# A two-block transformer layer: the units around each norm split into two halves of the tokens

## What is computed

```
def _rmsnorm_2(x, g):
    x32 = x.astype(jnp.float32)
    y = x32 * lax.rsqrt(jnp.mean(x32 * x32, axis=-1, keepdims=True) + RMS_EPS)
    return (y * g.astype(jnp.float32)).astype(x.dtype)
...
for l in range(DEPTH_2):
    g = norm_g[l]
    f = _swiglu(_rmsnorm_2(x, g[0]), ffn_w_gate[l, 0], ffn_w_up[l, 0], ffn_w_down[l, 0])
    x = x + 0.5 * _rmsnorm_2(f, g[1])
    m = _mixer(_rmsnorm_2(x, g[2]), w_in[l], conv_w[l], pool_w[l], pool_scale[l], w_out[l])
    x = x + _rmsnorm_2(m, g[3])
    f = _swiglu(_rmsnorm_2(x, g[4]), ffn_w_gate[l, 1], ffn_w_up[l, 1], ffn_w_down[l, 1])
    x = x + 0.5 * _rmsnorm_2(f, g[5])
```

## Time and profile before

| | before |
|---|---|
| median of 3 runs | 2515.86 us (2514.7 to 2516.48) |
| the profiled execution: its time | 2514.94 us |
| the profiled execution: its span | 2513.1 us |
| TensorE busy | 2475.0 us, 98% |
| VectorE busy | 1310.6 us, 52% |
| ScalarE busy | 908.9 us, 36% |
| GpSimd busy | 972.2 us, 39% |
| mean granted clock of TensorE | 0.994 |

### The profile page before, as it was taken

The page is one execution under the profiler, slowest core; times in us unless marked ns, Lnnn a source line. Parts: engine busy times, 40 slices in busy tenths (PEclk is TensorE's granted clock), DMA queues, the critical chain, the costliest instruction groups (busy, mean ns, idle before and its releaser), DMA issues.

```text
span 2513.1 us, 32584 instructions
## 1 busy us (share of the span) xinstructions
PE 2475.0 (98%) x11268; PEld 1980.1 (79%) x11268; DVE 1310.6 (52%) x1830; ACT 908.9 (36%) x1294; POOL 972.2 (39%) x384
## 2 busy tenths in 40 slices
PE   6999999999999999999999999999999999999998
PEld 3878778887788887778788888788887778788886
DVE  8865767256330348668531348430348668531344
ACT  3444543234321334554431333331334554431231
POOL 1332424443344443233344443344443333344443
PEclk8999999999999999999999999999999999999999
DMA  5222643322233231222233232233231322232232
GB/s 229 96 73 78 218 182 126 109 100 84 75 104 105 100 106 61 84 84 101 67 104 105 100 105 73 77 110 103 94 108 60 90 83 96 72 105 91 92 105 79
DMA packets 69702, 253.37 MB, mean 101 GB/s; under 512 B 8928, under 2 KB 11104, under 8 KB 68480
## 3 DMA queue, kind: packets, MB, share of 16 engines
q1 hardware_dynamic: 69632, 252.46, 29.8%
HBM read 244.76 MB, written 2.10 MB: 98 GB/s over the span
## 4 chain that ended last, share of the span: by engine, by line
PE 86%; issue 10%; POOL 2%; DVE 1%; DMA 0%; ACT 0%; SPq 0%; POOLq 0%; DVEq 0%; ACTq 0%
PE unit_bank L511 26%; PE unit_bank L513 26%; PE unit_bank L512 26%; PE score L597 3%; POOL w_lo L473 2%; PE mix L653 1%; PE out_bank L633 1%; PE score L902 1%; PE mix L553 0%; PE mix L661 0%; PE out_bank L558 0%; PE mix L558 0%; PE stat_bank L566 0%; PE score L653 0%; PE mix L566 0%
## 5 line engine op out<-in xcount | busy, mean ns | idle before, releaser
L473 POOL TENSOR_TENSOR w_lo<-raw,w_hi 128x1024 fp32r<-128x1024 f32 (+2 forms) x376 | 967.0, 2572 | 1519.9 <-ACT w_hi L950 1519.9
L511 PE MATMUL unit_bank<-u_hi,w_hi 128*128 128x512 f32 x2160 | 849.8, 393 | 4.0 <-POOL w_lo L473 4.0
L950 ACT ACTIVATE w_hi<-raw 128x1024 fp32r<-128x1024 f32 (+2 forms) x376 | 417.0, 1109 | 1202.2 <-PE unit_bank L513 1175.6
L513 PE MATMUL unit_bank<-u_hi,w_lo 128*128 128x512 f32 x2160 | 841.6, 390 | 0.0
L512 PE MATMUL unit_bank<-u_lo,w_hi 128*128 128x512 f32 x2160 | 841.6, 390 | 0.0
L511 PEld LDWEIGHTS unit_bank<-u_hi,w_hi 128*128 128x128 f32 x2160 | 405.7, 188 | 106.4 <-issue 16.0
L513 PEld LDWEIGHTS unit_bank<-u_hi,w_lo 128*128 128x128 f32 x2160 | 405.8, 188 | 85.1
L512 PEld LDWEIGHTS unit_bank<-u_lo,w_hi 128*128 128x128 f32 x2160 | 405.9, 188 | 84.7 <-issue 1.9
L511 PE MATMUL unit_bank<-h_hi,w_hi 128*128 128x512 f32 x992 | 387.0, 390 | 0.2 <-DVE h_lo L1765 0.2
L513 PE MATMUL unit_bank<-h_hi,w_lo 128*128 128x512 f32 x992 | 386.0, 389 | 0.0
L512 PE MATMUL unit_bank<-h_lo,w_hi 128*128 128x512 f32 x992 | 385.9, 389 | 0.0
(11 more groups left out here) (314 smaller groups left out, 1891.7 us busy)
## 6 DMA issues: line engine op xcount, KB each, us to landing
raw<-in_w_gate_up SPq DMA_DIRECT2D x168, 512.0 KB, 3.4
raw<-in_w_down SPq DMA_DIRECT2D x64, 704.0 KB, 4.1
raw<-in_w_in SPq DMA_DIRECT2D x66, 512.0 KB, 3.5
raw<-in_w_up SPq DMA_DIRECT2D x30, 512.0 KB, 3.4
f<-in_w_ada_rows SPq DMA_DIRECT2D x26, 512.0 KB, 4.9
raw<-in_w_out SPq DMA_DIRECT2D x24, 512.0 KB, 3.5
raw<-in_w_down SPq DMA_DIRECT2D x16, 512.0 KB, 3.5
ada_in_u<-in_w_ada SPq DMA_DIRECT2D x4, 1024.0 KB, 10.8
```

Of the source, the lines that this page charges most:

```text
L473: e.tensor_tensor(w_lo[:, s, 0:n], raw[:, s, 0:n], as32(w_hi[:, s, 0:n]), ALU.subtract).then_inc(lo_ready, 1)
L511: e.matmul(bank[:], wh, hi(k), start=n == 0, stop=False)
L513: mm = e.matmul(bank[:], wl, hi(k), start=False, stop=last)
L950: e.activation(w_hi[:, s, 0:n], raw[:, s, 0:n], ACT.Copy).then_inc(hi_ready, 1)
```

## The change

For the norms r = 0 to 5, the last pair of units of the stage and the first pair of the next are done in halves of 256 tokens. The last pair leaves the loop and becomes four half units of 3 × `n_k` matmuls of 256 columns, in the order (s, half) = (0, 0), (1, 0), (0, 1), (1, 1). The sums of half 0 stand ahead of (1, 1), and its spread inside it, behind 5 input chunks. The first pair of the next stage is 8 chunks of half 0 and then 8 of half 1, and the sums and the spread of half 1 stand among those of half 0. The takes, cross sums, squares, updates and gains of the last pair and of the whole update become two operations of half the width each. `keep_warm` goes. `u_lo`, the copies of weights and the last norm (r = 6) keep their full width. A scratch of the update moves from `unit_bank[1]` to `mix[1]`, since half 1's spread now lies in `unit_bank[1]`.

```diff
--- before.py
+++ after.py
+FSQ = 20
...
+        halves = (slice(0, T // 2), slice(T // 2, T))
+        scratch = (unit_bank[0], mix[1])
...
-            def norm(r):
-                ahead = r < NORMS - 1
-                e.wait_ge(fsq_added, (DC - 1) * (r + 1))
+            def unit_half(p, s, hf, r, n_k, at=None, insert=None):
+                cs = halves[hf]
+                if hf == 0:
+                    e.wait_ge(lo_ready, 2 * p + s + 1)
+                    e.wait_ge(taken[s], p + 1)
+                else:
+                    e.wait_ge(half_taken, 2 * r + s + 1)
+                for k in range(n_k):
+                    if k == at:
+                        insert()
+                    wh, wl = w_hi[:, s, k * P:(k + 1) * P], w_lo[:, s, k * P:(k + 1) * P]
+                    e.matmul(unit_bank[s][:, cs], wh, h_hi[:, k, cs], start=k == 0, stop=False)
+                    e.matmul(unit_bank[s][:, cs], wh, h_lo[:, k, cs], start=False, stop=False)
+                    mm = e.matmul(unit_bank[s][:, cs], wl, h_hi[:, k, cs], start=False, stop=k == n_k - 1)
+                mm.then_inc(unit_done if hf else half_done, 1)
+            def half_sums(hf, src, first):
+                for b in (2 * hf, 2 * hf + 1):
+                    mm = e.matmul(square_sum[:, b:b + 1], src[:, b * P:(b + 1) * P], tab("ones", 0, 1),
+                                  start=first and b == 2 * hf, stop=not first and b == 2 * hf + 1)
+                return mm
+            def half_spread(n, hf, bank):
+                e.wait_ge(inverse_ready, n)
+                for b in (2 * hf, 2 * hf + 1):
+                    mm = e.matmul(bank[:, b * P:(b + 1) * P], inv_f[:, b:b + 1].broadcast_to([P, P]), tab("ident"),
+                                  start=True, stop=True)
+                mm.then_inc(spread_ready, 1)
...
+            def norm(r, p, n_k):
+                unit_half(p, 0, 0, r, n_k)
+                unit_half(p, 1, 0, r, n_k)
+                unit_half(p, 0, 1, r, n_k)
+                e.wait_ge(fsq_added, DC * r + DC - 1)
+                half_sums(0, f_acc, True)
+                e.wait_ge(fsq_ready, FSQ * r + 15)
+                half_sums(0, f_sq, False).then_inc(sums_ready, 1)
+                unit_half(p, 1, 1, r, n_k, 5, lambda: half_spread(3 * r + 1, 0, stat_bank))
+                def pair(hf, c):
+                    e.wait_ge(u_full, 2 * DC * r + DC * hf + c + 1)
+                    for s in range(2):
+                        mm = e.matmul(score[s][:, halves[hf]], first_raw[:, s, c * P:(c + 1) * P],
+                                      u_all[:, c, halves[hf]], start=c == 0, stop=c == DC - 1)
+                        if hf and c == DC - 1:
+                            mm.then_inc(first_done, 1)
+                e.wait_ge(fsq_added, DC * r + DC)
+                half_sums(1, f_acc, True)
+                for s in range(2):
+                    e.wait_ge(first_loaded[s], 16 * (FIRST_OF_NORM + r + 1))
+                pair(0, 0)
+                pair(0, 1)
+                e.wait_ge(fsq_ready, FSQ * r + 19)
+                half_sums(1, f_sq, False).then_inc(sums_ready, 1)
+                pair(0, 2)
+                half_spread(3 * r + 2, 1, unit_bank[1])
+                pair(0, 3)
                 e.wait_ge(cross_ready, r + 1)
                 mm = token_sums(gf_sum, gf_acc)
                 if r:
                     mm = token_sums(cross_sum, cross_acc)
                 mm.then_inc(cross_sums, 1)
-                keep_warm(3)
-                for s in range(2):
-                    e.wait_ge(first_loaded[s], 16 * (FIRST_OF_NORM + r + 1))
+                for c in range(4, DC):
+                    pair(0, c)
                 for c in EIGHT:
-                    e.wait_ge(u_full, DC * r + c + 1)
-                    for s in range(2):
-                        mm = e.matmul(score[s][:], first_raw[:, s, c * P:(c + 1) * P], u_all[:, c, :],
-                                      start=c == 0, stop=c == DC - 1)
-                        if c == DC - 1:
-                            mm.then_inc(first_done, 1)
+                    pair(1, c)
                     if c == 6:
-                        spread(2 * r + 2, inv_u, mix[1])
+                        spread(3 * r + 3, inv_u, stat_bank)
...
+                for s in range(2):
+                    half_square(s, 0)
+                    half_gf_square(s, 0)
+                half_root(0)
+                half_square(0, 1)
+                half_gf_square(0, 1)
+                refill(p + 1, 0)
+                half_u(0, 0)
+                half_u(0, 1)
+                half_square(1, 1)
+                half_u_hi(0, 0)
+                half_u(0, 2)
+                half_root(1)
+                half_gf_square(1, 1)
+                half_u(0, 3)
+                half_u_hi(0, 1)
+                half_u_hi(0, 2)
+                half_u_hi(0, 3)
+                for c in range(4, DC):
+                    half_u(0, c)
+                    half_u_hi(0, c)
+                    if c == 4:
+                        refill(p + 1, 1)
                 for c in range(DC):
-                    e.wait_ge(x_ready, DC * r + c + 1)
-                    e.activation(u_all[:, c, :], x[:, c, :], ACT.Identity,
-                                 scale=col("norm_g", 2 * r * DC + c)).then_inc(u_full, 1)
-                    e.wait_ge(u_full, DC * r + c + 1)
-                    e.activation(u_hi[:, c, :], u_all[:, c, :], ACT.Copy).then_inc(uhi_ready, 1)
-                    if c == 1:
-                        refill(p + 1, 1)
-                    if c == 5:
+                    half_u(1, c)
+                    half_u_hi(1, c)
+                    if c == 4:
                         e.wait_ge(grown_ready, r + 1)
                         token_root(root_u, x_sum)
-                e.wait_ge(spread_ready, 2 * r + 2)
-                e.activation(rstd[:], mix[1][:], ACT.Copy).then_inc(rstd_ready, 1)
+                e.wait_ge(spread_ready, 3 * r + 3)
+                e.activation(rstd[:], stat_bank[:], ACT.Copy).then_inc(rstd_ready, 1)
...
+                half_take(0, 0)
+                half_cross(0, 0)
+                half_add(f_acc, f_sq, 13, 0)
+                half_add(gf_acc, gf_sq, 14, 0)
+                e.sem_inc(fsq_added, 1)
+                half_take(1, 0)
+                half_cross(1, 0)
+                half_add(gf_acc, gf_sq, 16, 0)
+                half_take(0, 1)
+                half_cross(0, 1)
+                half_inverse(0)
+                half_add(f_acc, f_sq, 17, 1)
+                half_add(gf_acc, gf_sq, 18, 1)
+                e.sem_inc(fsq_added, 1)
+                e.wait_ge(spread_ready, 3 * r + 1)
+                half_update(0, 0)
+                half_update(1, 0)
+                half_take(1, 1)
+                half_update(2, 0)
+                half_update(3, 0)
+                half_inverse(1)
+                half_cross(1, 1)
+                half_add(gf_acc, gf_sq, 20, 1)
+                e.sem_inc(cross_ready, 1)
+                for c in range(4, DC):
+                    half_update(c, 0)
+                e.wait_ge(spread_ready, 3 * r + 2)
                 for c in range(DC):
-                    update(c)
-                    if c == 3 and ahead:
+                    half_update(c, 1)
+                    if c == 1:
                         e.wait_ge(cross_sums, r + 1)
                         step(e.tensor_tensor(scaled, gf_sum, inv_f, ALU.mult))
@@ -1844,33 +2006,32 @@
                             e.tensor_tensor(x_sum, x_sum, grown, ALU.add).then_inc(grown_ready, 1)
                         else:
                             e.tensor_tensor(x_sum, scaled, inv_f, ALU.mult).then_inc(grown_ready, 1)
-                    if c == DC - 1 and ahead:
-                        e.wait_ge(root_ready, 2 * r + 2)
-                        e.reciprocal(inv_u, root_u).then_inc(inverse_ready, 1)
...
+                e.wait_ge(root_ready, 3 * r + 3)
+                e.reciprocal(inv_u, root_u).then_inc(inverse_ready, 1)
                 for c in range(DC):
-                    e.wait_ge(uhi_ready, DC * (2 + r) + c + 1)
+                    e.wait_ge(uhi_ready, 2 * DC + 2 * DC * r + DC + c + 1)
                     e.tensor_tensor(u_lo[:, c, :], u_all[:, c, :], as32(u_hi[:, c, :]),
                                     ALU.subtract).then_inc(u_ready, 1)
```

147 lines of the change are left out of this document (97 added, 50 removed).

## The result

| | before | after |
|---|---|---|
| median | 2515.97 us (6 runs, 2514.42 to 2517.27) | 2523.78 us (6 runs, 2523.29 to 2526.86) |
| the profiled execution: time, span | 2514.94, 2513.1 us | 2523.51, 2521.7 us |
| mean granted clock of TensorE | 0.994 | 0.993 |

The ratio of the runs is 1.0034, with a 95% interval of 1.0021 to 1.0047: slower by 7.8 us, beyond the 0.2% that a measurement can tell. The forecast was 2522.

The account below looks back on a forecast made before the run. TensorE's own order, busy 98% of the span, was taken as the bound. Norms +0.4, mixers +4.2 and clock +1.7 us made +6.3 on 2514.94, so 2521.2, median 2522; own range 2518 to 2527, overall 2509 to 2531.

Parts of the forecast that it names:

- The mixers' start: At r = 1 and 4, VectorE reaches `u_lo` and `q_st` late, delaying the DMA and first scores: +4.2 us for both.
- The clock: Behind TensorE's idle time ahead of the mixers' scores, one clock fall counted for both mixers: 1.7 us, bounds 0 and 3.4.
- Matmul of 256 columns: In the last pair's half units, each half matmul takes 0.120 us, against 0.227 for a full one.
- rival of fast halves: Half matmuls in the last pair take 0.111 us: 4.6 us less, 2516 with no clock fall, within 0.2%; chance 0.18.
- work term of −10.8: TensorE's own work over the six norm windows, without any wait, shrinks by 10.8 us.
- The waits for the weights and for the copy: In six norms, TensorE waits for GpSimd's weights (6.3 us) and ScalarE's copy in half 0 (3.1), within 11.2 of waits.
- The norms of 8 chunks: At r = 2 and 5: work −2.1, waits for weights 0.95, copy 0.5 and VectorE 0.75 us, about 0 at each.
- Nets +0.4 us: TensorE's way through the six norms: −10.8 us of work plus 11.2 of waits gives +0.4.
- The port: Rival at r = 2 and 5: VectorE's last addition waits for GpSimd's split, +4.6 us, 2527; chance 0.14 shared with dearer halves.

Follow-up runs that it names:

- Kernel 1: Changed kernel with VectorE scaling `q_st` and `k_st` behind the fifth chunk of `u_lo` at norms ahead of a mixer: median 2517.53 us, ratio 1.0007.
- Kernel 3: Changed kernel with GpSimd splitting only 128 columns of each stage's last unit, the other low parts left old and wrong: 2520.68 us, one run.
- Kernel 6: kernel 4 with the edits of Kernel 1 and 5, and VectorE's first-unit cross products behind the take of the second unit's half 0: median 2532.84 us.
- kernel 7: Kernel 6 with ScalarE's weight copy for GpSimd waiting until VectorE's addition behind the first inverse is done: 2516.23 us, one run.
- kernel 10: kernel 9 with the gate of kernel 7 and cross products moved only at norms of 8 chunks: median 2511.5 us, ratio to before 0.9984.
- 5: Kernel 1 with ScalarE's copy of the last weights moved from half 0 to behind the third chunk of half 1: median 2520.32 us, ratio 1.0015.
- kernel 8: Kernel 1 with three dummy matmuls ahead of (1, 0), and three ahead of (0, 1) at norms of 8 chunks: median 2517.37 us, ratio 1.0010.
- kernel 4: Changed kernel with only the last pair's second unit in halves, half 0's sums and spread inside (1, 1): median 2523.49 us, ratio 1.0032.
- kernel 2: Changed kernel with ten unread matmuls on TensorE in the wait ahead of each mixer's first scores: 2523.63 us, one run.
- kernel 9: The edits of Kernel 1 and kernel 4 together, nothing else: median 2515.46 us, ratio 1.0001.

## Why the prediction was right, and where it was not

- **The mixers' start: right to 0.1 us.** `u_lo` at 33.95 was measured at 33.99, the scores at 45.05 at 45.15 (1015.65 − 970.50). The term was +4.2; without the falls of the clock (1.65 each) the mixers grew by 2.0 and 2.1. Kernel 1 shows the cause by taking it away.
- **The clock: right in kind, half in number.** I counted one fall of 1.7 us, it fell behind both waits, 1.65 each: 1.6 us more. Both bounds of that term were in the range.
- **Matmul of 256 columns: 0.120, as taken.** That decides against the rival of fast halves and against the 0.109 us of the Trainium skill ("TensorE: Matmul & The Clock Gate", back-to-back issue gap and LDWEIGHTS). But the **work term of −10.8 left out a cost.** Window less waits should be 35.3, 31.0 and 30.15; the busy column has 35.80, 31.97 and 30.59: −6.9 in all. Part of these 3.9 us is missing work: the first matmul behind a wait takes 0.22 instead of 0.12 (0.20 behind the spread inside (1, 1)), and cutting the work in halves makes more such places. The larger part is bookkeeping: at each of the sixteen waits of the norms the busy column holds about 0.16 us of waiting, up to the modelled end.
- **The waits for the weights and for the copy: right.** The rows add up to 9.2 against the forecast's 11.2, but only because of those 0.16 us. By the starts the weights cost 1.11 and 0.91 us per norm against 1.15 and 0.95, and ScalarE's copy (0.35 in its row) 0.51 against 0.5. Kernel 3 finds 6.5 for the weights, with the slower first matmul, against 6.3. At the three norms of 11 chunks forecast and measurement are +0.15 and +0.21, at the first norm −0.35 and −0.39.
- **The norms of 8 chunks: the step that failed.** "Nets +0.4 us" was +2.2, and nearly all of that is r = 2 and 5, where I had −2.1 + 0.95 + 0.5 + 0.75 = +0.1 each and measured +1.06 and +0.91. VectorE's take of (0, 0) ends at t = 7.6, not 7.1, so TensorE's wait ahead of (0, 1) is 0.91 us by the starts and not 0.4. I left out the idle 0.41 us ahead of it, between the loop's last addition and the take, though the row of before has it too. The other half of the miss: these norms have four waits, and the slower first matmul behind each (0.1 us) wasn't in the sum. First VectorE before, then after:

```profile
1183.02 0.69 DVE L1870 COPY f<-unit_bank 128x512 f32<-128x512 f32 x1 [0.41 <-DVE arena L1799]
```

```profile
1184.93 0.69 DVE L1902 TENSOR_TENSOR arena<-arena 128x512 f32<-128x512 f32 x1
1186.04 0.42 DVE L2031 COPY f<-unit_bank 128x256 f32<-128x256 f32 x1 [0.41 <-PE unit_bank L590]
```

- **The port: a near miss.** I gave the addition 0.3 us of room ahead of the split, and at the third norm it had 0.35:

```profile
1192.03 0.86 DVE L1959 TENSOR_TENSOR arena<-arena 128x256 f32<-128x256 f32 x2
```

```profile
1192.81 2.37 POOL L479 TENSOR_TENSOR w_lo<-raw,w_hi 128x1024 fp32r<-128x1024 f32 x1 [10.24 <-ACT w_hi L1010]
```

  The second of the two additions starts at about 1192.46 and is through unharmed. Kernel 6 shows the price of losing the race: 2.1 us per addition (2.53 against 0.43), near the 2.3 that the forecast had from the earlier trace rows, and kernel 7 shows the cause by taking the collision away. That the changed kernel kept clear of it, by 0.35 us, was as the forecast said, with no margin to speak of.
- By the terms: 0.4, 4.2 and 1.7 were 2.2, 4.1 and 3.3, with −1.0 at the program's ends; 6.3 was 8.6. The median's 2523.78 is 1.8 above the forecast and well inside the range. Some of that closeness is luck: norms and clock together came out 3.4 us dearer than said, and the shorter start and end of the program, which nobody forecast, took 1.0 back in the profile.

## What to carry to other kernels

Ask of a split that lets two engines overlap what was queued behind the old order on the third one: here two scalings at the end of VectorE's row cost 7.8 us, more than the six norms gave in the best form found (2.6 us in kernel 10, its fall left aside), and moving them cost nothing. Before moving an operation, look at what GpSimd does at its new time, for one SBUF addition of 0.42 us there cost 2.5. A half pays only as long as the next weights are ready within it: keep one whole unit ahead.

## What the runs showed of the hardware that I had not expected

- With the unread matmuls gone, TensorE's clock falls now and then within a norm that is 90 to 98% busy, for 3.4 or 6.8 us: none in the profiles of before, after, 1, 5, 7 and 8 (after has the two in its mixers, and 3 and 4 have some there too), at one norm in 2 and 10, at two in 3, 4 and 9, at four in 6. A single one costs about 1.65 us, a double one in kernel 9 some 2.5 to 2.8 (37.11 and 36.76 against 34.3). Kernel 6, with the longest waits (2.61 and 3.31 us), has the most, but 3, which waits less than after, has two, and in kernel 10 the two waits ahead of the fall are 0.26 and 0.36 us. With dummies in two of the waits (kernel 8) three of eleven runs were still at 2520 to 2521.25. What sets one off in a given run stays open.
- The DMA that turns q and k can land later in one mixer than in the other, counted from the last pair's start: by 1.7 us in kernel 2 and by 1.2 in kernel 4. It is the landing and not the issue: in kernel 2 the first scores start 4.30 us behind the first of the four issues in one mixer and 6.02 us in the other, in kernel 4 4.40 and 5.57.
- In the changed kernel, half a matmul costs more than half: 0.12 against 0.227 when it follows its like, 0.22 when it comes first behind a wait.
- The collision of kernel 6 hits small operations too. In kernels 4 and 9 an operation on 4 columns takes 2.33 us at the first norm, where a split had begun 0.05 us before it (kernel 9 below). In kernel 10 the same operation begins 0.02 us ahead of the split and takes 0.16. The first norm's window is 31.15 in the two and 30.87 in kernel 10; whether that comes of it wasn't tested.

```profile
625.79 2.33 DVE L2002 TENSOR_TENSOR stat<-arena 128x4 f32<-128x4 f32 x1
```

```profile
625.74 2.36 POOL L481 TENSOR_TENSOR w_lo<-raw,w_hi 128x1024 fp32r<-128x1024 f32 x1 [5.60 <-ACT w_hi L1014]
```
